# Mix-out stage of a retention–convolution transformer: another order of DVE's and ACT's steps, and alternating PSUM banks for the last retention tiles

## What is computed

```python
p = modulate(x, sh1, sc1) @ w_in[l]                  # q, k, v, gate g, conv a and b
o_f, _ = retention_scan(q, k, v, lg_f, s_f)          # chunks of 128 tokens
o_b, _ = retention_scan(flip(q), flip(k), flip(v), lg_b, s_b)
# retention_readout, for o = o_f + flip(o_b), per head of 64
on = (o - mean(o)) * rsqrt(var(o) + eps) * gn_w + gn_b
ret = silu(g) * on
# conformer_conv: depthwise conv of width 31, then
conv = silu(layer_norm(u, ln_w, ln_b))
mix = concatenate([ret, conv]) @ w_out[l]
x = layer_norm(alpha * x + g1 * mix, ln1_w, ln1_b)
```

## Time and profile before

| | |
|---|---|
| runs | 2992.02, 2992.8, 2993.59 us (median 2992.8) |
| the profiled execution's own time | 2993.97 us |
| its span, first to last instruction | 2992.0 us |
| mean granted TensorE clock | 0.962 |
| busy share of PE, DVE, POOL, ACT | 92%, 64%, 36%, 24% |
| chain that ended last, by engine | PE 79%, DVE 8%, POOL 5%, DMA 4%, issue 2%, ACT 2% |

### The profile page before, as it was taken

One profiled execution on the slowest core, in us unless ns is written; L12 is line 12 of the kernel. 1 busy time (PEld: TensorE's weight loads), 2 busy tenths in 40 slices (PEclk: granted clock), 3 DMA queues, 4 the chain that ended last, 5 costly groups with the idle time before them and its releaser, 6 DMA issues.

```text
span 2992.0 us, 36849 instructions
## 1 busy us (share of the span) xinstructions
PE 2738.4 (92%) x13212; PEld 2227.6 (74%) x13212; DVE 1929.6 (64%) x3223; ACT 716.8 (24%) x1454; POOL 1066.4 (36%) x973
## 2 busy tenths in 40 slices
PE   5999898688999999999999599998688999999996
PEld 3777676467788888888888477786476888888885
DVE  4778785557667667767768888772655544544456
ACT  3222334433210110111111323334423111111111
POOL 1244354456111111111112645454563333332325
PEclk9999999799999999999999799999898999999998
DMA  8222222441122222222121211211522111111111
GB/s 240 88 78 69 87 83 77 136 127 36 47 73 71 70 79 75 70 72 83 56 45 35 82 55 59 61 48 33 158 64 64 49 49 49 45 53 42 53 45 63
DMA packets 246650, 214.59 MB, mean 72 GB/s; under 512 B 60384, under 2 KB 203280, under 8 KB 246544
## 3 DMA queue, kind: packets, MB, share of 16 engines
q10 hardware_dynamic: 139776, 117.46, 13.1%
q1 hardware_dynamic: 106768, 95.77, 10.7%
HBM read 190.56 MB, written 22.63 MB: 71 GB/s over the span
## 4 chain that ended last, share of the span: by engine, by line
PE 79%; DVE 8%; POOL 5%; DMA 4%; issue 2%; ACT 2%; SPq 1%; ACTq 0%; POOLq 0%; DVEq 0%
PE bank L528 14%; PE bank L530 14%; PE bank L529 14%; PE bank L1015 9%; PE bank L1016 9%; PE bank L1017 9%; PE bank L889 2%; PE bank L890 2%; PE bank L891 2%; PE bank L608 1%; PE bank L949 1%; PE bank L948 1%; PE bank L932 1%; DMA plain_words<-in_w_ada 1%; PE bank L939 1%
## 5 line engine op out<-in xcount | busy, mean ns | idle before, releaser
L1443 POOL TENSOR_TENSOR w_lo<-raw,w_hi 128x1024 fp32r<-128x1024 f32 x120 | 288.2, 2403 | 1114.0 <-ACT w_hi L1277 1114.0
L1015 PE MATMUL bank<-x_hl,w_hi 128*128 128x512 f32 (+1 forms) x1280 | 474.8, 371 | 0.0
L1016 PE MATMUL bank<-x_hl,w_hi 128*128 128x512 f32 (+1 forms) x1280 | 472.9, 369 | 0.0
L1017 PE MATMUL bank<-x_hl,w_lo 128*128 128x512 f32 (+1 forms) x1280 | 472.4, 369 | 0.0
L1716 DVE TENSOR_TENSOR work<-work,bank 128x512 f32<-128x512 f32 x576 | 390.0, 686 | 122.4 <-PE bank L530 111.5
L1692 DVE TENSOR_TENSOR work<-work 128x512 f32<-128x512 f32 (+1 forms) x160 | 158.0, 987 | 471.1 <-ACT work L1265 471.0
L528 PE MATMUL bank<-w_hi,h_hi 128*128 128x512 f32 x1152 | 450.7, 391 | 7.2 <-DVE work L1716 5.3
L529 PE MATMUL bank<-w_lo,h_hi 128*128 128x512 f32 x1152 | 448.9, 390 | 0.0
L530 PE MATMUL bank<-w_hi,h_lo 128*128 128x512 f32 x1152 | 448.8, 390 | 0.0
L1616 DVE SCALAR_TENSOR_TENSOR bank<-work,bank 128x512 f32<-128x512 f32 (+1 forms) x580 | 407.2, 702 | 18.9
L1277 ACT ACTIVATE w_hi<-raw 128x1024 fp32r<-128x1024 f32 x120 | 126.8, 1059 | 783.7 <-PE bank L530 585.3
(11 more groups left out here) (141 smaller groups left out, 4392.6 us busy)
## 6 DMA issues: line engine op xcount, KB each, us to landing
raw<-in_w_ff ACTq DMA_DIRECT2D x128, 512.0 KB
work<-in_w_ada SPq DMA_DIRECT2D x48, 512.0 KB
raw<-in_w_in ACTq DMA_DIRECT2D x64, 256.0 KB
plain_words<-in_w_ada ACTq DMA_DIRECT2D x64, 256.0 KB
raw<-in_w_in ACTq DMA_DIRECT2D x16, 512.0 KB
plain_words<-in_w_ada SPq DMA_DIRECT2D x16, 512.0 KB, 12.2
raw<-in_w_out ACTq DMA_DIRECT2D x16, 512.0 KB
gate_rows<-work SPq DMA_DIRECT2D x72, 64.0 KB, 1.6
```

Of the source, the lines that this page charges most:

```text
L1015: nc.tensor.matmul(o, slot(mlp_slot(l, f), 0)[:, wc], x_hi[:, k, cols], start=k == 0, stop=False)
L1016: nc.tensor.matmul(o, slot(mlp_slot(l, f), 0)[:, wc], x_lo[:, k, cols], start=False, stop=False)
L1017: mm = nc.tensor.matmul(o, slot(mlp_slot(l, f), 1)[:, wc], x_hi[:, k, cols], start=False, stop=k == KT - 1)
L1443: nc.gpsimd.tensor_tensor(slot(mlp_slot(l, sl), 1), raw[:, un % 2, :], slot(mlp_slot(l, sl), 0).bitcast(F32), ALU.subtract).then_inc(w_rea ...
```

## The change

It has two parts. In mix-out, DVE does the shift and scaling of tile st-1 right behind the centring of tile st, then the low part of tile st-2, and the variance of tile st last; tile 0 is centred, measured and scaled ahead of the loop. ACT's turn becomes: gate swish of tile st-1, convolution swish and high part of tile st-2, square of tile st, normalised convolution part of tile st-1. In the retention tail, the steps planned from the second turn after the last projection on (`late`) alternate banks: scores use banks 0 and 1, values banks 2 and 3, so each waits for the tile before the last one. These are all 10 tiles of the last head pair in the first layer, and in the second layer 7 of 8 for scores and 8 of 8 for values. PE's, POOL's and SP's orders of work stay as they are.

```diff
@@ mix_in_plan @@
+            late = n > len(steps) + 1
             following = [x for x in ready if x not in scored][:1]
             for x in following:
-                plan.append(("scores", *x))
+                plan.append(("scores", *x, late))
                 scored.add(x)
             for p, t in now:
-                plan.append(("values", p, t))
+                plan.append(("values", p, t, late))
@@ banks @@
-        ps_sc, ps_o = banks[5][:, 0:2 * P], banks[6]
+        def ps_scores(r, late):
+            return (banks[r % 2] if late else banks[5])[:, 0:2 * P]
+        def ps_values(r, late):
+            return banks[2 + r % 2] if late else banks[6]
@@ PE, scores @@
-                        if r:
+                        if late:
+                            pe.wait_ge(S["evac_q"], s0["evac_q"] + n * PAIRS)
+                            pe.wait_ge(S["prob_done"], s0["prob_done"] + r - 1)
+                        elif r:
                             pe.wait_ge(S["prob_done"], s0["prob_done"] + r)
@@ PE, values @@
-                        if r:
+                        if late:
+                            pe.wait_ge(S["evac_q"], s0["evac_q"] + n * PAIRS)
+                            pe.wait_ge(S["conv_op"], s0["conv_op"] + 4 * TAPS * len(chunks_of(l)))
+                            pe.wait_ge(S["comb_b"], s0["comb_b"] + r - 1)
+                        elif r:
                             pe.wait_ge(S["comb_b"], s0["comb_b"] + r)
@@ ACT, mix-out @@
                 for st in range(n + 2):
-                    if st < n:
-                        act.wait_ge(S["g_in"][st % 2], s0["g_in"] + 16 * (st // 2 + 1))
-                        nc.scalar.activation(g_in[:, st % 2, :], g_in[:, st % 2, :], ACT.Silu).then_inc(S["silu_g"], 1)
-                        act.wait_ge(S["gn_cent"], s0["gn_cent"] + st + 1)
...
                     j = st - 1
                     if 0 <= j < n:
-                        act.wait_ge(S["cn_shift"], s0["cn_shift"] + j + 1)
...
+                        act.wait_ge(S["g_in"][j % 2], s0["g_in"] + 16 * (j // 2 + 1))
+                        nc.scalar.activation(g_in[:, j % 2, :], g_in[:, j % 2, :], ACT.Silu).then_inc(S["silu_g"], 1)
                     j = st - 2
...
                         last.then_inc(S["mix_hi"], 1)
+                    if st < n:
+                        act.wait_ge(S["gn_cent"], s0["gn_cent"] + st + 1)
+                        if st:
+                            act.wait_ge(S["gn_var"], s0["gn_var"] + st)
+                        nc.scalar.activation(sq, X[:, T[st], 0:512], ACT.Square).then_inc(S["sq_done"], 1)
+                    j = st - 1
+                    if 0 <= j < n:
+                        act.wait_ge(S["cn_shift"], s0["cn_shift"] + j + 1)
+                        nc.scalar.activation(X[:, T[j], 512:D], banks[4 + j % 2][:, :], ACT.Identity,
+                                             bias=shift[:, j % 2, :], scale=rs[:, j % 2, :]).then_inc(S["cnorm"], 1)
@@ DVE, mix-out: the same instructions, now in functions @@
+                centre(0)
+                variance(0)
+                scale_heads(0)
+                for st in range(1, n + 4):
+                    if st >= 4:
+                        combine(st - 4)
+                    if st < n:
+                        centre(st)
+                    if 2 <= st <= n:
+                        scale_heads(st - 1)
+                    if 2 <= st < n + 2:
+                        low_part(st - 2)
+                    if st < n:
+                        variance(st)
```

More of the change, by code:

```diff
@@ L734, in _ @@
                     if a[0] == "values":
-                        _, p, t = a
+                        _, p, t, late = a
                         r = row_of(l, p, t)
@@ L1582, in _ @@
                             dve.wait_ge(S["comb_done"], s0["comb_done"] + r)
+                        ps_o = ps_values(r, late)
                         by_dir = inter.rearrange("p (h d e) -> p h d e", h=2, d=2)
@@ new lines, in combine @@
+                def combine(j):
+                    if j == 0:
+                        dve.wait_ge(S["rows_in"], s0["rows_in"] + 64)
+                    dve.wait_ge(S["z_done"], s0["z_done"] + j + 1)
+                    dve.wait_ge(S["res_in"][j % 2], s0["res_in"] + 16 * (j // 2 + 1))
+                    z = banks[2 + j % 2][:, :]
+                    link(nc.vector.tensor_tensor(z, z, gate_row[:, cond_of(T[j]), :], ALU.mult))
+                    nc.vector.scalar_tensor_tensor(X[:, T[j], 0:512], X[:, T[j], 0:512], ALPHA, z, ALU.mult, ALU.add).then_inc(S["z_read"], 1)
@@ new lines, in centre @@
+                def centre(j):
+                    par = j % 2
+                    o, mean, _, _ = heads_of(j)
+                    dve.wait_ge(S["o_in"][par], s0["o_in"] + 16 * (j // 2 + 1))
+                    link(nc.vector.tensor_reduce(mean, o, AX.X, ALU.add))
+                    link(nc.vector.tensor_scalar(mean, mean, 1.0 / DK, None, ALU.mult))
+                    nc.vector.tensor_tensor(o, o, mean.unsqueeze(2).to_broadcast([P, HEADS, DK]), ALU.subtract).then_inc(S["gn_cent"], 1)
+                    dve.wait_ge(S["cvt_done"], s0["cvt_done"] + j + 1)
+                    link(nc.vector.bn_stats(bn[:, par, 0:6], banks[4 + par][:, :]))
+                    link(nc.vector.bn_aggr(mv[:, par, :], bn[:, par, 0:6]))
+                    nc.vector.tensor_scalar(mv[:, par, 1:2], mv[:, par, 1:2], EPS, None, ALU.add).then_inc(S["cn_var"], 1)
@@ new lines, in low_part @@
+                def low_part(j):
+                    dve.wait_ge(S["mix_hi"], s0["mix_hi"] + j + 1)
+                    cols = slice(T[j] * P, (T[j] + 1) * P)
+                    for half in range(2):
+                        last = nc.vector.tensor_tensor(x_lo[:, 4 * half:4 * half + 4, cols], banks[half][:, :].rearrange("p (a b) -> p a b", b=P),
+                                                       x_hi[:, 4 * half:4 * half + 4, cols].bitcast(F32), ALU.subtract)
+                    last.then_inc(S["mix_lo"], 1)
@@ new lines, in variance, with scale_heads @@
+                def variance(j):
+                    _, _, var, _ = heads_of(j)
+                    dve.wait_ge(S["sq_done"], s0["sq_done"] + j + 1)
+                    link(nc.vector.tensor_reduce(var, sq.rearrange("p (h e) -> p h e", h=HEADS), AX.X, ALU.add))
+                    nc.vector.tensor_scalar(var, var, 1.0 / DK, EPS, ALU.mult, ALU.add).then_inc(S["gn_var"], 1)
+                def scale_heads(j):
+                    o, _, _, rstd = heads_of(j)
+                    dve.wait_ge(S["cn_pow"], s0["cn_pow"] + j + 1)
+                    nc.vector.scalar_tensor_tensor(shift[:, j % 2, :], mv[:, j % 2, 0:1], -1.0, rs[:, j % 2, :], ALU.mult, ALU.mult).then_inc(S["cn_shift"], 1)
+                    dve.wait_ge(S["gn_pow"], s0["gn_pow"] + j + 1)
+                    nc.vector.tensor_tensor(o, o, rstd.unsqueeze(2).to_broadcast([P, HEADS, DK]), ALU.mult).then_inc(S["gn_norm"], 1)
```

59 lines of the change are left out of this document (8 added, 51 removed).

## The result

| | before | after |
|---|---|---|
| median of the runs made together | 2992.43 us (4 runs, 2992.02 to 2993.59) | 2972.85 us (4 runs, 2972.05 to 2973.65) |
| the profiled execution's own time | 2993.97 us | 2972.73 us |
| its span | 2992.0 us | 2970.7 us |
| mean granted TensorE clock | 0.962 | 0.962 |

The change gains 19.6 us by the medians; the ratio of the times is 0.9923, with an interval of 0.9909 to 0.9937. The prediction was 2970 us, between 2962 and 2981, with 0.94 for faster. A second comparison of the same two kernels, `after_again`, gave 2973.79 against 2995.41 us: 0.9926 (0.9913 to 0.9940).

The account below looks back on a forecast made before the run. Mix-out was taken as bound by two equally long rings of waits, the tail by its own bank ring. Gains of 10.9 + 6.4 + 4.0 + 1.2 = 22.5 us gave a 2970 us median, range 2962 to 2981.

Parts of the forecast that it names:

- Both rings of the old turn: Mix-out: two equally long rings of waits, through the gate (9.94 us) and through the low part (9.43 us).
- B: Mix-out's old ring from one low part to the next, 9.43 us, with DVE waiting 2.73 us for ACT's high part.
- The ring of two turns: New mix-out: transposes, projection, combine, centring, scaling and POOL's products sum to 15.4 us, so 7.7 a turn.
- 0.25 for POOL's lock: Mix-out: DVE's centring delays POOL's power by 0.5 us in about every second turn, so 0.25 a turn.
- The rival in which the loads set the turn at 8.75: Mix-out: columns landing 1.5 us later make the turn 8.75 and give back 8 us, 2978 us; chance 15%.
- That PE alone counts (7.2): Mix-out rival: two-turn ring cut, POOL's lock nothing, a turn 7.2 us, 6 us more gain, 2964 us; chance 15%.
- eight of 9.0: Mix-out rival: late variance holds power and scaling, turns of 9.0 us, 2983 us in all; chance 5%.
- The term of 10.9: First layer's mix-out: last gate product ends at 634.9 instead of 645.75, a gain of 10.9 us.
- tile 3 ends at 2143.83, now 1.4 earlier: Second layer's mix-out: tile 3's gate product comes 1.4 us earlier, part of a 6.4 us gain.
- tiles 31 and 32 gain 0.55 each: First layer's retention tail: with alternating banks, PE's work sets the pace and these tiles gain 0.55 us each.
- That stretch keeps its length: First layer's retention tail: the steps where stores land late among six loads gain nothing.
- The slower rival (PE's clock): Mix-out: PE stays at its lower clock level, a turn takes 13.3 us, 3050 us in all; chance 3%.

Follow-up runs that it names:

- swish_only: The kernel before with only ACT's gate swish moved a turn later; 2990.12 us against 2994.46, ratio 0.9987.
- order_only: The change's mix-out order with the gate swish back in its own turn and the tail's old banks; 2983.50 us against 2994.46 before, ratio 0.9961.
- dve_swish: The kernel before with DVE's new order and the late gate swish, ACT's square and normalised part still ahead of the high part; 2989.98 us, ratio 0.9986.
- no_eps: The full change without DVE's L1677, leaving out the 1e-5 added to the heads' variance; 2969.91 us, ratio 0.9917 to the kernel before.
- mid_eps65: The change with DVE's combine behind centring and scaling, and L1677 replaced exactly by a 65th column holding 1e-5; 2965.16 us, ratio 0.9899 to before.
- t_only: The kernel before with only the retention tail's alternating banks, mix-out in its old order; 2990.68 us against 2994.46, ratio 0.9985.
- combine_mid: The full change with DVE's combine behind centring and scaling, residual load waiting for the load two tiles before; 2965.96 us, ratio 0.9897 to before.
- loads_late: The full change with the six loads of mix-out's first two tiles issued behind the last retention store; 2969.01 us, ratio 0.9914 to before.
- all_three: The change with combine behind scaling, L1677 replaced by a 65th column, and six loads behind the last tail store; 2963.62 us, ratio 0.9888 to before.

## Why the prediction was right

**The rings.** Both rings of the old turn were read rightly: the waits for gate rows are gone, and `swish_only`, `order_only` and `dve_swish` show that each of them, where it is left, holds the turn back: B keeps it at 9.3 to 9.4 us, the gate load keeps every second turn at 9.7.

**What is late next.** The ring of two turns was forecast at 15.4 us and measures 15.30 to 15.42 in three of four cases, once 15.92. With 0.25 for POOL's lock the turn was put at 7.95; the five turns from tile 3 to tile 8 take 7.32, 8.09, 8.28, 7.32 and 8.10, a mean of 7.82.

That this lies near 7.95 is in part luck, because the term of 0.25 was wrong. It stood for POOL's power of eight columns, which was to be held up by DVE's centring in every second turn; in the change none of these 18 powers takes longer than 1.80 us, and their median is 1.65. That lock appears in `no_eps` (2.01 us, once in each layer), not here. The one that the change does have, POOL holding up DVE's L1677, was not in the sum.

What lengthens the mean from 7.7 to 7.82 are, as far as the rows show, columns that came late: the transposes of 593.28 start 1.13 us behind their gate product. The prediction put 5.74 us between the end of the transposes and the taking of the columns; there it is 6.80, by the slow issue of the rows, and 5.68 and 6.05 in two later turns. The execution of `after_again` has a mean of 7.64.

The rival in which the loads set the turn at 8.75 did not come: they come late in single turns, and the worst is 1.06 us over the 5.74 of before and not 1.5. That PE alone counts (7.2) did not come either; it takes `mid_eps65` to get to 7.11. The prices of two rivals do not follow from the prediction's own terms: eight turns of 8.75 instead of 7.95 are 6.4 us and not 8, and eight of 9.0 are 8.4, so about 2978 and not 2983.

**First layer.** From tile 3's gate product to the last 46.7 us were forecast and 46.06 measured, and that product came 1.36 us earlier behind the tail than before, where 1.4 was forecast. The term of 10.9 measured 11.5. The 1.36 is luck: the first gate product came 2.0 us earlier, which was not forecast and which `t_only` has too, and the three turns behind it took 0.6 us longer than before, where the new order was to shorten them by 1.4.

**Second layer.** 30.75 us were forecast and 29.64 measured, 1.1 better; but the product of tile 3 came 0.8 later behind the tail, where 1.4 earlier was forecast. The three turns up to it take 9.59, 9.18 and 10.28 us, against 9.42, 9.51 and 9.42 before. The step that failed is "tile 3 ends at 2143.83, now 1.4 earlier". The prediction let the first combine start right behind the low part of tile 1, as before. In the new order the variance stands between the two, and then DVE is at the combine ahead of the projection and waits for it; the scaling stands behind the combine, as it did before, and waits too.

```profile
2116.01 1.29 DVE L1668 TENSOR_TENSOR x_hl<-bank,x_hl 128x512 fp32r<-128x512 f32 x2 [2.39 <-ACT x_hl L1247]
2117.22 0.68 DVE L1676 TENSOR_REDUCE work<-work 128x8 f32<-128x512 f32 x1
...
2119.31 0.70 DVE L1647 TENSOR_TENSOR bank<-bank,work 128x512 f32<-128x512 f32 x1 [1.22 <-PE bank L537]
```

From the low part to the combine are 3.30 us here, against 1.20 before (2133.05 to 2134.25). From the combine to the end of tile 3's gate product are 8.71, as the 8.76 of the forecast has it. The prediction set the variance and DVE's wait for PE at nothing in this turn, in both layers. `combine_mid` shows what they were worth: without the combine ahead of the scaling this turn is 7.11 us in the first layer (9.95 in the change) and 8.08 in the second (10.28); in `mid_eps65` it is 8.50 and 7.12.

**The tail.** 4.0 and 1.2 us were forecast and 2.2 and -0.1 measured. The mechanism (the ring is doubled, then stores pin the steps) was right, the sizes not. Even of the 2.2 more than half may belong to this one execution of the kernel before: the five kernels with the old banks and the loads among the stores have first tails of 23.64 to 25.83 us, 24.4 on average, the six with the alternating banks 22.38 to 24.35, on average 23.4.

The step "tiles 31 and 32 gain 0.55 each" failed by the clock: a step is 1.32 us at the upper level, better than the 1.5 of the sum, but the first two steps of the change run at the lower level and take 2.56 and 2.47, longer than the 2.05 of before, which ran at a granted clock of 0.93 to 1.00 (with the old banks, `swish_only` has a step of 2.95 at a granted clock of 0.50). The first four steps together take 7.67 us instead of 8.20. "That stretch keeps its length" failed the other way: the two steps with stores take 6.67 instead of 5.57 us, the last three 5.29 instead of 7.48. In the second layer the stores take back all: DVE stands 3.23 and 1.09 us for them. The prediction assumed that a store lands at a fixed time whatever the pace; with a faster pace the store whose buffer is wanted is issued while the loads are still being issued, and it holds up DVE for longer.

**The sum.** 22.5 us were forecast by the executions' own times, 21.2 came (2993.97 to 2972.73): the two stretches that were over-estimated by 4.2 us together (tails 3.1, second mix-out 1.1) are balanced by 0.6 in the first mix-out and 2.4 in stretches in which nothing was changed. So part of the closeness is luck of the execution. By the medians 22.8 us were forecast and 19.6 came.

The slower rival (PE's clock) did not come. The transposes of the mixed rows after, ns min/median/max, beside the earlier trace rows:

```profile
L996 PE MATMUL bank<-work x80: 272/273/421, 557.7 to 631.8; 128*128 128x128 f32 x80
```

The median is 273 ns as before, and the granted clock between 584 and 626 us is 1.00.

## What to carry to other kernels

When two rings of waits are equally long, opening one shows only a part of the gain (4 and 11 of 20 us here); look for the operations that each ring passes on each engine, and expect the whole gain only when the last of them is moved. Then write down the longest ring in the new order with durations from the old trace, over two turns if buffers alternate: here its 7.7 us lie within 2% of the 7.82 measured. What such a sum misses is the start and the end, where a wait (for the first projection, for a store that is issued among loads) takes back what the steady turns do not show.

## What the runs showed of the hardware

**A tiny DVE instruction can cost 1 us beside POOL.** In the change the scalar operation on 128x8 (L1677) takes 0.93 us at 582.59 and ends at 583.52; POOL's product on 128x512 (L1401) runs from 582.22 to 583.49. Where nothing of POOL runs it takes 0.17 (546.01). It has only one SBUF input. Larger, with a DVE instruction that has two SBUF inputs:

```profile
556.94 2.91 DVE L1657 TENSOR_TENSOR work<-work 128x512 f32<-128x512 f32 x1
```

```profile
556.94 2.36 POOL L531 TENSOR_TENSOR h_lo<-raw,h_hi 128x1024 fp32r<-128x1024 f32 x1
```

DVE's subtraction of the head means, 0.69 us long at 565.63, starts here with POOL's 2.36 us instruction and takes 2.91. The prediction weighed this lock only on its way from DVE to POOL. The Trainium skill ("SBUF — State Buffer", Who interferes with whom) says that whoever comes first holds the shared ports for its whole instruction, and that a scalar operation can take both ports in its fast mode. Both pairs of rows agree with the first: DVE's instruction ends 0.03 us behind POOL's in the one, and 0.55 behind it in the other. That L1677 ran in the fast mode no run shows. And the rule does not hold beside every instruction of POOL: the scalar operation of the same shape in the centring (L1656) takes its 0.17 us at 585.48, in the middle of POOL's power on 128x8 (585.31 to 586.96), and so it does at all eleven places of the change where the two meet. Here the measurement decides: a small DVE operation waits for POOL's wide instructions, not for its power.

**The clock in the tail.** In the first layer's tail the granted clock falls to 0.50 to 0.53 in every version looked at and rises at different places: it is 0.93 over 524 to 527 us before, 0.52 there in the change, and 1.00 from 521 on in `loads_late`. TensorE is busy for all of the 3 us from 521 to 524 in both of the first two. A step at the lower level costs 1.1 to 1.2 us more. Why it rises later in the change was not settled: `all_three` and `loads_late`, with the same edit of the tail, differ in it too.
